# A two-block layer on one core: the first mixer reordered, its state-space chain ahead of the retention part

## The chip, the core and the metric

The kernel runs on one NeuronCore of a Trainium2 chip. A core has a matrix engine (TensorE, PE in the profile, with its weight loads as a row of their own, PEld), a vector engine (VectorE, DVE), an activation engine (ScalarE, ACT), a general engine (GpSimd, POOL) and a queue that issues DMAs (SyncE, SP). Each runs its own program in order, and they meet at semaphores. SBUF has 128 partitions and holds everything that is not in DRAM; products land in PSUM, eight banks of 128 x 512 float32. The metric is the time of one execution on the device in microseconds (us).

## The reference, cut to what matters

The whole is two transformer blocks over 1024 tokens of width 1024, in float32. Only the first block's mixer is touched in its order:

```python
h = x @ w_in                              # 1024 x 2048: u | q,k | v | gate, 512 columns each
# state-space part (s5): 32 groups of 16 channels, 64 complex states each
bu = einsum(u, b_bar);  states = scan(lam_bar, bu);  y = real(einsum(states, c)) + d * u
y = gelu(y);  y_s5 = rms_norm(y * sigmoid(y @ glu_w + glu_b))
# retention part: 4 heads, rotary q and k, a decayed state from chunk to chunk
y_ret = group_norm(intra + cross) * silu(gate)
mix = concat(y_s5, y_ret) @ w_out         # then layer norm, a conv-gated FFN, layer norm
```

After it come, unchanged, the first FFN and the second block (differential attention, two gated linear attentions, branch products, an FFN of 4096).

## The kernel before, in words

Every large product is done in three passes of reduced precision: an operand is cut into a high part (ACT, a copy to float32r) and a low part (POOL for weights, DVE for activations, a subtraction), and high x high, high x low and low x high are summed in PSUM. Weights come as 241 units of 128 x 1024 (512 KB) in the order of `weight_plan` (L52). A unit passes three places: SP loads it into a ring of NRAW = 3 raw slots (`load`, L2224), ACT cuts its high part (`act_cut`, L911, line L918) and POOL its low part (`pool_cut`, L2045, line L2050) into a ring of NSPL = 6 slots. Unit v may be cut when unit v - NSPL has been used up, and each program has its calls `act_cut(e, done)`, `pool_cut(e, done)` and `load(e, done)` at fixed places: they go up to unit done + NSPL (for `load` done + NSPL + NRAW).

A product is of one of two kinds. `pe_feature` (L371) turns one unit into 128 output features of all tokens: 48 matmuls of 128 x 512 into two banks. `pe_token_block` (L389) keeps four units at hand (two in the FFN's second half) and runs through the eight blocks of 128 tokens, 24 matmuls each; only in the last of the eight are its units given free. Banks are handed out round robin by `claim` (L353): whoever takes a bank waits until its last reader is done.

The first mixer runs in stages. `pe_in` (L419) makes u with four features and then three token blocks, qk, v and g (gate). DVE copies u out (L1388), and SP stores it to DRAM (`ubuf`). ACT copies qk and v out and applies silu to g, and all three stay in SBUF whole (QK, VV, GG, 16 KB of each partition each). Beside this DVE computes the state-space tables from L1393 on: exponentials and the angle arguments, on which ACT's two sines wait in order behind the eight copies of qk (L939, L940); powers PP, the input matrices BBR, and the rotation table ET.

Then comes `pe_retention` (L436) with `dve_retention` (L1466), a software pipeline of twelve steps: step n rotates q and k of chunk n on DVE (`keys`), turns them on PE (flip, L416), makes scores of chunk n - 1, outputs of chunk n - 2 (L460, L463) and the state's increment (L470); DVE masks (`masked`, L1502, L1507), updates the state (`state`, L1518), normalizes (`norm`, L1526 to L1540), and the result is turned (rt, L416) and cut into XH and XL (L1555).

After the last turn come `pe_s5` (L490), `dve_s5` (L1558), `act_s5` (L960), `pool_s5` (L2106) and `sp_s5` (L2256): DVE expands B by powers (M, BB, six operations of 128 x 2048), POOL does the same for C (C, CL, 24 operations of 128 x 576); PE turns B, injects u (L505), DVE rotates and scans (RTMP, WW) and rotates back (N, SS); PE makes the convolution kernel (L518), ACT copies it to KT, POOL adds d, SP spreads it into the Toeplitz tile T8 by eight DMAs (L2267); PE makes y with T8 and the states (`y8`, L530, L532), 24 matmuls in the program for each of four parts; ACT applies gelu, SP sends it through DRAM to turn its layout (`ybuf` L2271, YP L2274). Then the glu products (L367 with GH, GL), sums of squares (L554), the root and the scaling (L1626 to L1637). `pe_project_out` (L602) starts with the two weight units of the retention half (L618), so that the scaling of the state-space half runs beside it.

Of the kernel before, what the change touches and what calls it, by code (L numbers as in the profile page):

```python
# [7 lines left out]
F = mybir.dt.float32  # L8
# [8 lines left out]
NRAW = 3  # L17
NSPL = 6
KB = 1024
BASE = 1152 + 8 * KB  # L20
# [166 lines left out]
def build(nc, D, out):  # L187
    plan, order1, order2 = weight_plan()
    with ExitStack() as ctx:
# [3 lines left out]
        def sem(name):  # L193
# [14 lines left out]
        trig_arg, trig = sem("angles_reduced"), sem("sines_done")  # L208
        r_rot, r_qx, r_y, r_hi = (sem(n) for n in ("ret_rotated", "ret_query_scaled", "ret_normed", "ret_high_cut"))
        s_bk, s_cl, s_bb, s_et, s_t8z, s_kd, s_ss = (sem(n) for n in (  # L210
            "s5_b_kept", "s5_c_powers", "s5_b_powers", "s5_tables_read", "s5_toeplitz_zero", "s5_kernel_done", "s5_states"))
# [25 lines left out]
        WR = sb("WR", -8, [128, NRAW, 1024])  # L237
        WH = sb("WH", 4, [128, NSPL, 1024], R)
        WL = sb("WL", 28, [128, NSPL, 1024], R)
# [14 lines left out]
        U8 = sb("U8", 52, [128, 32, 128])  # L254
        QK = sb("QK", 148, [128, 8, 512])
        VV = sb("VV", 164, [128, 8, 512])
        GG = sb("GG", 180, [128, 8, 512])
        RT = sb("RT", 196, [128, R_N])
        GNG = sb("GNG", 202, [128, 512])
        TA = [sb(f"TA{j}", 84 + j, [128, 8, 32]) for j in range(4)]  # L260
        KQT = sb("KQT", 88, [128, 2, 4, 128])
        QX = sb("QX", 92, [128, 2, 2, 128])
        PT = sb("PT", 94, [128, 2, 4, 128])
        KZ = sb("KZ", 58, [128, 3, 256])
        SR = sb("SR", 52, [128, 2, 256])
        YR = sb("YR", 54, [128, 2, 512])

        ET = sb("ET", 116, [128, 16, 2, 128])
# [8 lines left out]
        CL = sb("CL", 148, [128, 16, 2, 144])  # L277
        BB = sb("BB", 166, [128, 16, 2, 128])
        SS = sb("SS", 84, [128, 16, 2, 128])
        BBT = sb("BBT", 182, [128, 16, 2, 128])  # L280
        KT = sb("KT", 84, [16, 32, 128])
        WW = sb("WW", 166, [128, 16, 2, 128])
        Y8 = sb("Y8", 116, [128, 32, 128])
        M1 = sb("M1", 84, [128, 16, 128])
        M2 = sb("M2", 92, [128, 16, 128])
        C1 = sb("C1", 142, [128, 4, 144])
        C2 = sb("C2", 144.5, [128, 4, 144])
        BK = sb("BK", 202, [128, 2, 16, 16])
        DM = sb("DM", 198, [16, 32])
        RTMP = sb("RTMP", 199, [128, 2, 2, 128])  # L290
        LAM = sb("LAM", 201.5, [128, 16])
        N1 = sb("N1", 182, [128, 16, 128])
        N2 = sb("N2", 190, [128, 16, 128])
        YP = sb("YP", 116, [128, 4, 1024])
        GH = sb("GH", 148, [128, 4, 1024], R)
        GL = sb("GL", 164, [128, 4, 1024], R)
        SG = sb("SG", 182, [128, 2, 1024])
        RS = sb("RS", 190, [128, 2, 1024])
# [90 lines left out]
        def pe_token_block(e, name, unit, col, row0, tiles, xh, xl, slots, after=None):  # L389
            vs = [wt.next(unit, row0 + 128 * k, 2, col, 512) for k in range(0, tiles, 2)]  # L390
            for i in range(8):
# [18 lines left out]
                u.units = wt.done  # L410
                if after:
                    after(i)

# [5 lines left out]
        def pe_in(e):  # L419
# [12 lines left out]
            pe_token_block(e, "qk", "w_in", 512, 0, 8, XH, XL, range(8))  # L432
            pe_token_block(e, "v", "w_in", 1024, 0, 8, XH, XL, range(8))
            pe_token_block(e, "g", "w_in", 1536, 0, 8, XH, XL, range(8))

        def pe_retention(e):  # L436
            def scores(i):
                d = i % 2
                f = lots["flip", i]
# [34 lines left out]
            for n in range(12):  # L474
# [4 lines left out]
                if n < 8:  # L479
                    u = claim(e, ("flip", n))  # L480
                    e.wait_ge(r_rot, n + 1)
                    if n == 0:
                        e.wait_ge(cst, 32)
# [6 lines left out]
        def pe_s5(e):  # L490
            for q in range(8):
                u = claim(e, ("bbt", q))
                if q == 0:
                    e.wait_ge(s_bb, 1)
# [2008 lines left out]
```

## Time and profile before

| | us |
|---|---|
| median of 3 runs | 3565.62 (3564.34 to 3565.73) |
| the profiled execution | 3569.1 |
| its span | 3567.2 |
| PE busy in the span | 3149.6 (88%) |
| PE on the chain that ended last | 80% |
| DVE on it | 9% |
| POOL busy | 996.8 (28%) |
| DVE busy | 1251.4 (35%) |

The profiled execution lies 3.5 us above the median. The profile's page cuts the span into 40 slices of 89.2 us. Its PE digits begin 8, 9, 5, 3, 5, 5, 8 and are 7 or more from there on, and the granted clock of TensorE falls to 5 tenths in the fifth and sixth of them. "Granted clock" is the share of full speed that the chip gave TensorE: 0.50 is 1.2 GHz, 1.00 is 2.4 GHz. Rows of the timeline begin with start and duration; what stands in brackets behind them is the idle time of the engine just before and what ended it. Where an operation's duration comes from a row with a count, it is the row's time by its count.

### The profile page before, as it was taken

To read this page: it belongs to the slowest core of one execution; us is meant where nothing else is said; L and a number is where in the kernel's file an instruction comes from. 1 tells how busy PE (TensorE), PEld (TensorE's weight loads), DVE (VectorE), ACT (ScalarE), POOL (GpSimd) and SP (SyncE) were. 2 spreads that over 40 slices of the span, in tenths; PEclk is the share of its full clock that TensorE was granted. 3 is DMA by queue.
4 is the path that set the end of the run, shared out by engine and by line. 5 is a ranking of instruction groups with operands and counts; after the bars stand their busy time and mean duration, and the time that the engine had idled before them with its cause. 6 is when DMAs were issued, how large, how long until landed. Compare 5 with 4: busy or idle time off the path is not lost.

```text
span 3567.2 us, 35327 instructions
## 1 busy us (share of the span) xinstructions
PE 3149.6 (88%) x14706; PEld 2578.5 (72%) x14706; DVE 1251.4 (35%) x2356; ACT 871.3 (24%) x1258; POOL 996.8 (28%) x446
## 2 busy tenths in 40 slices
PE   8953558999999998987899788799999999999995
PEld 7742346888888886665677677678887878888884
DVE  3567415321221225446345544511122511111115
ACT  2211012322112113333333444411112321111211
POOL 2214101543223234210133222212221453333332
PEclk9976569999999998998999999999999999999998
DMA  4102122111111111201111100022112111111101
GB/s 165 48 24 24 14 53 89 48 48 48 60 47 54 48 43 52 79 30 36 36 36 36 36 30 30 24 89 71 54 48 100 36 53 59 51 51 48 48 30 47
DMA packets 60351, 180.33 MB, mean 51 GB/s; under 512 B 9472, under 2 KB 18064, under 8 KB 60176
## 3 DMA queue, kind: packets, MB, share of 16 engines
q1 hardware_dynamic: 60192, 178.07, 16.2%
q8 instruction: 117, 1.92, 0.2%
q14 instruction: 42, 0.34, 0.0%
HBM read 157.99 MB, written 18.87 MB: 50 GB/s over the span
## 4 chain that ended last, share of the span: by engine, by line
PE 80%; DVE 9%; ACT 4%; issue 3%; POOL 3%; DMA 1%; SPq 1%; POOLq 0%; DVEq 0%; ACTq 0%
PE PS L367 44%; PE PS L400 7%; PE PS L402 7%; PE PS L401 7%; PE PS L578 3%; PE PS L818 2%; PE PS L416 1%; PE PS L707 1%; POOL WL L2050 1%; PE PS L532 1%; DVE s L1345 1%; PE PS L618 1%; POOL DD L2175 1%; PE PS L530 1%; PE PS L735 1%
## 5 line engine op out<-in xcount | busy, mean ns | idle before, releaser
L2050 POOL TENSOR_TENSOR WL<-WR,WH 128x1024 fp32r<-128x1024 f32 x241 | 579.1, 2410 | 2218.7 <-ACT WH L918 2218.4
L367 PE MATMUL PS<-XH,WH 128*128 128x512 f32 x2176 | 692.2, 400 | 15.0 <-DVE XL L1384 12.3
L367 PE MATMUL PS<-XL,WH 128*128 128x512 f32 x2176 | 679.0, 394 | 0.0
L367 PE MATMUL PS<-XH,WL 128*128 128x512 f32 x2176 | 674.9, 392 | 0.0
L367 PEld LDWEIGHTS PS<-XH,WH 128*128 128x128 f32 x2176 | 405.5, 191 | 103.9 <-issue 21.2
L367 PEld LDWEIGHTS PS<-XL,WH 128*128 128x128 f32 x2176 | 414.8, 191 | 88.5
L367 PEld LDWEIGHTS PS<-XH,WL 128*128 128x128 f32 x2176 | 412.4, 190 | 88.0
L918 ACT ACTIVATE WH<-WR 128x1024 fp32r<-128x1024 f32 x241 | 253.1, 1056 | 808.2 <-PE PS L402 475.0
L400 PE MATMUL PS<-WH,HH 128*128 128x512 f32 x864 | 339.5, 393 | 14.4 <-POOL HL L2082 14.4
L401 PE MATMUL PS<-WL,HH 128*128 128x512 f32 x864 | 338.7, 392 | 0.0
L402 PE MATMUL PS<-WH,HL 128*128 128x512 f32 x864 | 338.6, 392 | 0.0
L1723 DVE TENSOR_TENSOR XF<-XF,PS 128x512 f32<-128x512 f32 x192 | 132.0, 687 | 342.1 <-PE PS L402 342.1
L1707 DVE TENSOR_TENSOR CT<-CT,PS 128x1024 f32<-128x1024 f32 x54 | 66.0, 1221 | 459.1 <-ACT CT L1052 310.9
L400 PEld LDWEIGHTS PS<-WH,HH 128*128 128x128 f32 x864 | 164.1, 190 | 49.8 <-POOL HL L2082 15.7
L401 PEld LDWEIGHTS PS<-WL,HH 128*128 128x128 f32 x864 | 164.0, 190 | 34.2
L402 PEld LDWEIGHTS PS<-WH,HL 128*128 128x128 f32 x864 | 163.7, 189 | 34.3
L2082 POOL TENSOR_TENSOR HL<-CT,HH 128x1024 fp32r<-128x1024 f32 x54 | 129.4, 2396 | 16.1 <-ACT HH L1058 16.1
L400 PE MATMUL PS<-WH,XH 128*128 128x512 f32 x320 | 125.3, 392 | 4.9 <-POOL WL L2050 4.9
L402 PE MATMUL PS<-WH,XL 128*128 128x512 f32 x320 | 124.6, 389 | 0.0
L401 PE MATMUL PS<-WL,XH 128*128 128x512 f32 x320 | 124.5, 389 | 0.0
L818 PE MATMUL PS<-KQ 64*128 64x128 f32 (+1 forms) x896 | 89.4, 286 | 29.3 <-DVE KQ L1942 23.6
L818 PEld LDWEIGHTS PS<-KQ 64*128 64x128 f32 (+1 forms) x896 | 84.7, 198 | 38.8 <-issue 30.2
(317 smaller groups left out, 3819.0 us busy)
## 6 DMA issues: line engine op xcount, KB each, us to landing
WR<-in_weights SPq DMA_DIRECT2D x241, 512.0 KB, 3.6
BR<-brbuf SPq DMA_DIRECT2D x12, 512.0 KB, 4.7
RAWX<-in_xT SPq DMA_DIRECT2D x8, 512.0 KB, 9.3
RES<-in_x SPq DMA_DIRECT2D x8, 512.0 KB, 7.7
xbuf<-XF SPq DMA_DIRECT2D x8, 512.0 KB, 2.8
brbuf<-STG SPq DMA_DIRECT2D x8, 512.0 KB, 2.6
RES<-xbuf SPq DMA_DIRECT2D x8, 512.0 KB, 7.2
out<-XF SPq DMA_DIRECT2D x8, 512.0 KB, 2.6
```

The costliest lines, as they stand in the source:

```text
L367: last = e.matmul(PS[:, u.b + h, :], w, x[:, k, 512 * h:512 * h + 512], start=k == 0 and w is w1 and x is xh, stop=k == nk - 1 and w is w2)
L400: e.matmul(PS[:, u.b, :], a, wh[:, k, :], start=j == 0 and k == 0, stop=False)
L401: e.matmul(PS[:, u.b, :], a, wl[:, k, :], start=False, stop=False)
L402: last = e.matmul(PS[:, u.b, :], c, wh[:, k, :], start=False, stop=j == len(vs) - 1 and k == 1)
L416: last = e.transpose(PS[:, u.b, 128 * j:128 * j + 128], src(j), ident[:, :])
L578: last = e.matmul(PS[:, u.b + h, :], w[:, k, :], x[:, k, 512 * h:512 * h + 512], start=k == 0 and w is wh and x is XH, stop=k == 7 and w i ...
L818: last = e.matmul(PS[:, us[g][hh].b, 128 * (i % 4):128 * (i % 4) + 128], kl[rows[hh], c], kr[rows[hh], c], start=True, stop=True)
L918: e.activation(WH[:, v % NSPL, :], WR[:, v % NRAW, :], ACT.Copy).then_inc(w_hi, 1)
L1707: e.tensor_tensor(X, X, bank(u, 2), ALU.mult).then_inc(u.drained, 1)
L1723: e.tensor_tensor(x, x, bank(u), ALU.add).then_inc(u.drained, 1)
L2050: e.tensor_tensor(WL[:, v % NSPL, :], WR[:, v % NRAW, :], WH[:, v % NSPL, :].bitcast(F), ALU.subtract).then_inc(w_lo, 1)
L2082: e.tensor_tensor(HL[:, v % 5, :], CT[:, v % 2, :], HH[:, v % 5, :].bitcast(F), ALU.subtract).then_inc(f_lo, 1)
```

## The change

- The ring of cut weights has NSPL = 5 slots in place of 6, in the whole kernel. The 8 KB of each partition that come free hold two staging tiles (STQ), the retention tables and other small tiles.
- qk, v and g no longer stay in SBUF. ACT copies each block of 128 tokens into one of two slots of STQ, and SP stores it to DRAM (`spill`, 24 pieces of 256 KB). In the retention SP brings them back by chunks into QKC (2 slots), VVC (3) and GGC (2).
- In the start SP issues one weight unit ahead of x in place of three, and the state-space tables right behind x. ACT copies u out, and the sines follow the third part of u. DVE goes on from XL straight to the tables, BB (now in four groups of 128 x 512 operations) and ET; POOL expands C as soon as the powers are there (`pool_powers`).
- PE's program is one, `pe_mixer`: u, six token blocks of qk, four turns of B, a block, four turns, the last block; kernel and injection products with blocks of v between; the four y products with blocks of v between. B's turned form is written back over BB, and WW and SS use the same tile, so DVE works in place in groups; y is written over U8. The kernel goes to DRAM by quarters (`ktbuf`) and from there into T8.
- The retention pipeline runs last. In its steps lie the last two v blocks (step 0), the eight g blocks (steps 1 to 8), the glu products (steps 5, 6, 8, 9) and their squares (two steps later). DVE's order in a step is norm, keys, masked, the cut of rt, state. `norm` has 4 + 4 operations with the gain and the gate (tiles GNG and GGC) in place of 4 + 1, and the product of gate and gain over all eight blocks goes.
- `pe_token_block` is built on `pe_token_steps`, which yields after each token block; elsewhere it issues what it issued.

The core of the diff:

```diff
-NSPL = 6
+NSPL = 5
...
+            qk = pe_token_steps(e, "qk", "w_in", 512, 0, 8, XH, XL, range(8))
+            tick(qk, 6)
+            for q in range(4):
+                turn_b(q)
+            tick(qk, 1)
+            for q in range(4, 8):
+                turn_b(q)
+            finish(qk)
+            values = pe_token_steps(e, "v", "w_in", 1024, 0, 8, XH, XL, range(8))
+            kernel_of(0)
+            inject(0)
+            inject(1)
+            kernel_of(1)
+            tick(values, 1)
+            kernel_of(2)
+            kernel_of(3)
+            for q in range(2, 8, 2):
+                inject(q)
+                inject(q + 1)
+                if q < 6:
+                    tick(values, 1)
+            for q in range(4):
+                outputs(q)
+                if q < 3:
+                    tick(values, 1)
...
+                if n == 0:
+                    finish(values)
+                else:
+                    tick(gates, 1)
+                if n in glu_at:
+                    p = glu_at[n]
+                    if p % 2 == 0:
+                        glu_units.append(wt.next("s5_glu_w", 0, 4, 128 * p, 256))
+                    glu(p)
+                if n - 2 in glu_at:
+                    squares(glu_at[n - 2])
+        glu_at = {5: 0, 6: 1, 8: 2, 9: 3}
...
+        def act_spill(e, name, i, func=ACT.Copy):
+            s = 8 * ("qk", "v", "g").index(name) + i
+            if s >= 2:
+                e.wait_ge(spilled[s % 2], 16 * (s // 2))
+            act_evac(e, lots[name, i], STQ[:, s % 2, :], func=func)
...
+            def kernel_of(p):
+                u = lots["kt", p]
+                k = KTS[p % 2]
+                if p >= 2:
+                    e.wait_ge(kt_out[p % 2], 16)
+                elif p:
+                    e.wait_ge(s_et, 1)
...
+            s = lots["y8", 3]
+            e.wait_ge(s.full, s.nfull)
+            qk(0)
+            qk(1)
+            e.wait_ge(s.drained, s.ndrained)
...
         def vector_program(e):
             dve_in(e)
+            dve_s5(e)
             dve_retention(e)
-            dve_s5(e)
```

The first `kernel_of` is PE's, the second ACT's: ACT's copy of the second quarter waits for `s_et`, the end of ET on DVE, since its tile lies over ET's scratch.

## Rows read from the trace of the kernel before

**Rows 1.** Windows: bounds, length, busy us (count) of PE, PEld, DVE, ACT, POOL; granted clock.

```profile
196.00:317.00 121.00, 52.75 (x252) 42.35 (x252) 94.45 (x317) 13.30 (x20) 10.38 (x5) 0.69 0.06 18
317.00:336.00 19.00, 0.10 (x1) 0.14 (x2) 18.76 (x8) 0.63 (x1) 18.54 (x6) 0.50 1.16 97
...
414.00:474.00 60.00, 59.66 (x192) 45.55 (x192) 0.08 (x1) 3.26 (x6) 0.00 (x0) 0.50 0.00 1
```

**Rows 2.** Waits of PE, 196 to 600 us: sum, times, longest.

```profile
PE PS L530 <- DVE SS L1613: 33.9, 1, 33.9
PE PS L367 <- DVE GL L1616: 27.5, 1, 27.5
```

**Rows 3.** Timeline of DVE, from the third part of u to the first rotation.

```profile
47.69 2.03 DVE L1388 COPY UP<-PS 128x1024 f32<-128x1024 f32 x1 [8.84 <-PE PS L367]
...
112.47 0.07 DVE L1410 MEMSET PP<- 128x16 f32 x1 [40.64 <-ACT LL L940]
...
123.76 0.29 DVE L1345 COPY BBR<-E 128x256 f32<-128x256 f32 x1
...
127.35 0.23 DVE L1345 MEMSET ET<- 128x16 f32 x2 [0.16 <-DVE LL L1345]
...
150.44 2.74 DVE L1345 TENSOR_TENSOR ET<-ET,E 128x512 f32<-128x512 f32 x1
...
158.42 2.88 DVE L1372 TENSOR_TENSOR E<-ET,LL 128x512 f32<-128x512 f32 x1
...
164.24 0.43 DVE L1345 COPY ET<-E 128x512 f32<-128x512 f32 x1
...
196.68 0.42 DVE L1345 TENSOR_TENSOR TA<-QK,RT 128x256 f32<-128x256 f32 x1
```

**Rows 4.** Timeline of ACT, a cut of x, a block of qk, the table load before the sines.

```profile
11.11 1.06 ACT L932 ACTIVATE XH<-RAWX 128x1024 fp32r<-128x1024 f32 x1 [0.21 <-DMA RAWX<-in_xT]
...
69.45 0.60 ACT L922 ACTIVATE QK<-PS 128x512 f32<-128x512 f32 x1 [4.84 <-PE PS L402]
...
110.79 1.28 ACT L939 ACT_TABLE_LOAD   x1
```

**Rows 5.** Timeline of POOL, four weight cuts, then the expansion of C.

```profile
149.87 10.89 POOL L2050 TENSOR_TENSOR WL<-WR,WH 128x1024 fp32r<-128x1024 f32 x4 [36.62 <-ACT WH L918]
...
317.23 3.32 POOL L2115 TENSOR_TENSOR C<-BCT,PP 128x576 f32<-128x576 f32 x1 [110.00 <-DVE XL L1555]
...
337.09 1.22 POOL L2115 TENSOR_TENSOR C<-BCT,PP 128x576 f32<-128x576 f32 x1
```

**Rows 6.** Timeline of DVE, the expansion of B, one group of scans, the rotation back.

```profile
322.73 3.18 DVE L1345 TENSOR_TENSOR BB<-M,M 128x2048 f32<-128x2048 f32 x1
...
343.57 0.42 DVE L1345 TENSOR_TENSOR RTMP<-PS,ET 128x256 f32<-128x256 f32 x1 [6.53 <-PE PS L505]
...
363.01 1.80 DVE L1345 TENSOR_TENSOR_SCAN WW<-LAM,WW 128x128 f32<-128x128 f32 x4
...
400.14 0.09 DVE L1345 MEMSET SS<- 128x32 f32 x1 [12.92 <-DMA T<-KT]
400.26 4.58 DVE L1345 TENSOR_TENSOR N<-WW,ET 128x2032 f32<-128x2032 f32 x2
```

**Rows 7.** Timeline of SP, the eight DMAs that fill T8 (issue).

```profile
384.79 8.95 SPq L2267 DMA_DIRECT2D T<-KT  x8
```

**Rows 8.** Timeline of DVE, two steps of the retention.

```profile
262.63 0.69 DVE L1555 TENSOR_TENSOR XL<-PS,XH 128x512 fp32r<-128x512 f32 x1 [1.97 <-ACT XH L958]
...
268.41 0.89 DVE L1526 BATCH_NORM_STATS2 s<-PS 128x6 f32<-128x128 f32 x4
```

**Rows 9.** Timeline of PE, a sum of squares, the projection's first product.

```profile
514.35 3.78 PE L554 MATMUL PS<-SG,ones 128*128 128x512 f32 x4 [5.06 <-DVE SG L1622]
...
560.40 1.42 PE L618 MATMUL PS<-WH,XH 128*128 128x512 f32 x1
```

**Rows 10.** Waits of PE from 100 to 200 us.

```profile
PE PS L400 <- POOL WL L2050: 4.9, 4, 1.8
```

More of the change, by code:

```diff
@@ L410, in pe_token_block @@
                 u.units = wt.done
+                yield
+        def pe_token_block(e, name, unit, col, row0, tiles, xh, xl, slots, after=None):
+            steps = pe_token_steps(e, name, unit, col, row0, tiles, xh, xl, slots)
+            for i in range(8):
+                next(steps)
                 if after:
                     after(i)
+            next(steps, None)
         def pe_turn_four(e, u, src):
@@ new lines, in inject @@
+            def inject(q):
+                t = lots["bbt", q]
+                e.wait_ge(t.drained, t.ndrained)
+                if q == 0:
+                    e.wait_ge(u8_in, 128)
+                u = claim(e, ("inj", q))
+                for j in range(4):
+                    gp, ri = 2 * q + j // 2, j % 2
+                    for g2 in range(2):
+                        last = e.matmul(PS[64 * g2:64 * g2 + 64, u.b, 128 * j:128 * j + 128],
+                                        BB[:, gp, ri, 64 * g2:64 * g2 + 64], U8[:, 2 * gp + g2, :], start=True, stop=True)
+                last.then_inc(u.full, 1)
@@ new lines, in kernel_of @@
+            def kernel_of(p):
+                u = claim(e, ("kt", p), 2)
+                e.wait_ge(s_cl, p + 1)
+                for gp in range(4 * p, 4 * p + 4):
+                    for g2 in range(2):
+                        rr, c0 = slice(64 * g2, 64 * g2 + 64), 128 * (gp % 4)
+                        for ri in range(2):
+                            last = e.matmul(PS[0:16, u.b + g2, c0:c0 + 128], BBR[rr, ri, gp, :], CL[rr, gp, ri, 0:128],
+                                            start=ri == 0, stop=ri == 1)
+                last.then_inc(u.full, 1)
@@ L934, in act_in @@
             for p in range(4):
[L935 to L944 removed]
+                u = lots["u", p]
@@ L1624, in dve_s5 @@
+                if 2 <= n < 9:
+                    state(n - 2)
+                if n == 4:
+                    for p in range(4):
+                        e.wait_ge(g_hi, p + 1)
+                        e.tensor_tensor(GL[:, p, :], YP[:, p, :], GH[:, p, :].bitcast(F), ALU.subtract).then_inc(g_lo, 1)
+                if n - 1 in glu_at:
+                    glu(glu_at[n - 1])
+            r0, r1, r2 = (RS[:, k, :] for k in range(3))
             u = lots["ss"]
@@ L2278, in sp_s5 @@
+            load(e, lots["g", 7].units)
+            load(e, lots["glu", 3].units)
+            e.wait_ge(g_sum, 4)
+            e.wait_ge(lots["ro", 7].full, lots["ro", 7].nfull)
             for i in range(8):
```

630 lines of the change are left out of this document (329 added, 301 removed).

## The prediction

> **What bounds the kernel now.** I read the profile's page first: PE is busy 88% of the span and carries 80% of the chain that ended last, so the kernel as a whole is bound by matmuls that the change doesn't touch. The exception is the first mixer: the page's digits for PE sink to 3 to 5 there and the granted clock with them. Then I read the windows by stage [rows 1]: in the 121 us of the retention PE works 52.8 us, in the 19 us in which DVE and POOL expand B and C it works 0.1, and in the 60 us of the y products it works all the time, but at a granted clock of 0.50. The waits of PE name the two longest idle stretches [rows 2]: 33.9 us for DVE's rotation and the Toeplitz tile, 27.5 us for y on its way through DRAM. The projection starts at 560.4 [rows 9]. Its own tail (root and scaling beside the two retention units) is the same before and after, so what the change is worth is how much earlier the projection's first product comes, less what the ring of five costs behind it.
>
> What could stand in that time: the 24 token blocks of qk, v and g take 5.44 us each (0.60 busy and 4.84 idle of ACT's copy [rows 4]), 131 us, and in the kernel before nothing but DVE's tables runs beside them. The retention and the state-space part are independent of each other. So the gain has a source: in one, DVE's chain of the state-space part moves beside qk and v; in the other, g, glu and the squares move into the retention, whose steps leave PE half idle.
>
> **Start.** x arrives in pieces 1.27 us apart (1.06 busy and 0.21 idle for one cut of x [rows 4]), each the size of a weight unit. Two weight units move behind x: everything starts 2 x 1.27 = 2.5 us earlier. The third part of u is complete at 47.7 before [rows 3], so at 45.2; ACT's strided copy is put at DVE's 2.0 us for it [rows 3], a weight cut at 1.1, the table load at 1.3 [rows 4], two sines at 0.4: DVE has the sines at about 50 in place of 112.5. It waited 40.6 us for them before [rows 3], because they stood behind the copies of qk on ACT; its argument work of some 11 us ends by 35 and is hidden.
>
> **Tables, B and C.** From the sines to BBR DVE takes 112.5 to 124.05 [rows 3], 11.6 us: done at 61.6. POOL first cuts unit 8 (which waits for the last part of u) and begins C at about 62. Then DVE's 24 operations of 128 x 512 and POOL's 24 of 128 x 576 run at once, and both read two operands from SBUF. The rows show what that costs: DVE's BB takes 3.18 us beside POOL and 2.29 alone for nearly the same size (4.58 for two [rows 6]), and POOL's C takes 3.32 beside DVE and 1.22 alone [rows 5]. They take turns: a pair takes about 3.2, 0.3 less than the sum of both alone. For a pair here I take 0.7 + 1.3 - 0.25 = 1.75 us, 42 us for all 24, with ends of 17 (DVE undisturbed, 24 x 0.72) and 47 (24 x 1.95, the full sum). BB is ready at 103.5. PE has done six blocks of qk by 89 and waits for the third and fourth group of B, up to about 8 us, which is hidden as long as DVE is the later one.
>
> The Trainium skill says the same more strictly, in SBUF — State Buffer, section "SBUF: two separate sides": a DVE operation with two SBUF inputs and a GpSimd operation exclude each other for their whole length. By it the pair is the full sum, 47 us in place of 42, 5 us more in the result. It speaks against putting DVE's and POOL's expansions side by side with ET behind them.
>
> The end of ET: squarings 3.3 us (124.05 to 127.35) and ET from 127.35 to 164.67 [rows 3], 37.3 us, of which four weight cuts of POOL took some 8.4 us (four operations from 150.44 to 158.42 took 2.5 to 2.9 us where the same forms take 0.4 to 0.7 [rows 3, 5]). The cuts of v's units, behind the last block of qk, fall into ET again, so I keep 37.3. **ET ends at E = 103.5 + 3.3 + 37.3 = 144.**
>
> **From E to y.** A group of the scans costs DVE 4.4 us (six operations at 0.42 and scans 1.80 [rows 6]), the rotation back of two groups six operations at 0.7: 8 x 4.4 + 4 x 4.4 = 53 us, the last at E + 53. The Toeplitz tile is later at first: ACT's second kernel copy waits for E and stands ahead of v's first copy; PE's fourth kernel quarter takes the banks of the first two injections (E + 5.5 to E + 9 at half clock); copy, d, store to DRAM (about 2 us each) end at E + 14; POOL clears T8 (3.5 us), SP stands behind the store of v's second block (E + 21), and from the first of the eight issues to landing it took 400.1 - 384.8 = 15.4 us [rows 6, 7]: T8 is there at E + 37. Then four y products with three v blocks between. Before they take 15 us each, at a clock of 0.50 throughout [rows 1]. The v blocks raise the clock (token blocks run at 5.44 us, full clock). I take 15 for the first, 11 for the others, between 7.5 and 15, and 6.5 for a v block: 15 + 33 + 19.5 = 67.5. **y is complete at E + 105 = 249**; the first chunk is fetched only then (its tile lies over C), 3 us: the retention starts at 252 in place of 196.7.
>
> The Trainium skill, TensorE: Matmul & The Clock Gate, the section on the HAM clock gate, says that activity releases the throttle. By it a stretch as busy as y's would run at the full clock, 30 us for the four and not 48, 18 us less in the result. The trace disagrees: 59.66 of 60 us busy at 0.50 [rows 1]. A v block between them is new, so that price is open on both sides.
>
> **The retention.** Before it takes 196.7 to 317.2 [rows 3, 5], 121 us, a step 13.6 us (249.07 to 262.63 [rows 8]), bound by DVE, with 2 us of idle for the turned result. Added: (1) the last two v blocks ahead of the first scores (10.9) and the first g block, which waits for units cut only after them, while SP, in `load`, waits for the same cuts and holds back the third chunk of qk (4), less 4 that hides: 11. (2) `norm` has three more operations on 128 x 128, +0.9 us per step for eight steps, mostly given back by the new order, which leaves no idle for the turned result: 5. (3) GL, four operations of 1.24: 5. (4) glu gates and squares on DVE, 8 of 1.24: 10. (5) PE's steps with g (5.4), glu (5.4) and squares (3.8 [rows 9]) pass DVE's 14 us in five steps, by some 2 to 4: 12. (6) six more weight cuts beside DVE, 2 us each: 9. Sum 52: **172 us, the projection at 252 + 172 = 424** in place of 560.4, 136 us earlier. Spills add 24 stores and 24 loads of 256 KB to SP; each wait there (a store behind ACT's copy, a chunk behind `state` or `norm`) is a step ahead of its use, so I cost them at nothing beyond (1); without that cover each chunk costs about 3 us, 24 us in eight steps.
>
> **The ring of five.** It counts in the whole kernel. At the starts of v and g PE waited 4.9 us in all for low cuts [rows 10], since a block gives its four units free only at its end. One slot less brings that to about 2.5 us where there was just enough: the second half of the first projection, one feature of the last FFN's start. Elsewhere, holding each cut's end against the unit's first use, the cut after it would still be in time by over 2 us. I take 5 us, between 0 and 15.
>
> **Sum.** 3569.1 - 136 + 5 = 3438 for an execution like the profiled one. That lies 3.5 us above the median, which I keep as the difference: **3435 us.**
>
> **The rivals.**
> (a) The gain is larger: DVE is less disturbed by POOL (up to 25), T8 isn't last, y runs at full clock (18), the retention costs 25 less since PE's extra work hides. Half of that: 3435 - 50 = 3385. For it speaks that PE is half idle in the retention; against it that pairs take turns in every row.
> (b) The retention becomes bound by PE at half clock or by SP's chunks: eight g steps at 20 us for 14, 48 us, and y at 15 throughout (12): 3495. For it speaks the clock of 0.69 in the retention [rows 1]; against it that g blocks keep PE dense.
> (c) Slower than before: the ring of five. If each change between token blocks behind the mixer (28 in the two FFNs, 4 in the projections) waited for a cut as v and g do, at 2.5 us, that would be 80 us; the sign turns where each costs 131 / 32 = 4.1 us or more, at 6 us 3620. Against it: an FFN block has two units, and three slots stay ahead.
> (d) The change doesn't do what it says: DVE runs in order, and the retention can't begin before the scans end. If the state-space chain took as long as before from the start of B (317 to 474, 157 us, from 62), y would be complete at 219 and not later: so order alone can't undo it. Its price is inside (b).
>
> **How the numbers follow.** Forecast 0.60, (a) 0.17, (b) 0.19, (c) 0.03, no change that can be told 0.01. About 0.2% is what a measurement of this kernel can tell from none. The forecast's own bounds: B and C -25/+5, y -18/+12, retention -25/+30, ring -5/+10, added as independent: -40/+35. The range goes on to (a) and halfway to (b): 3385 to 3485. Faster 0.96, same 0.01, slower 0.03.
>
> **What would show it.** Right: the first projection product at 415 to 435; the sines at 50; the last ET copy at about 144; BB operations at 0.7 busy but 1.7 apart; PE idle from about 120 to 145 and again before y; T8 landed near 180; y complete near 250; steps of 14 to 16 us. Wrong: y products at 7.5 us (a); steps of 20 us or DVE waiting for chunks (b); PE waiting on WL in the FFNs (c). If PE's waits behind the projection grew by over 15 us, or the projection began beyond 460, the sum is wrong.

## The result, and the profile after

| | before | after |
|---|---|---|
| median | 3565.51 us (3564.34 to 3565.73) | 3409.55 us (3408.32 to 3412.85) |
| the profiled execution | 3569.1 | 3408.3 |
| its span | 3567.2 | 3406.2 |
| mean granted clock of the profiled execution | 0.935 | 0.958 |

The changed kernel takes 0.9565 of the time of the one before (95% interval 0.9548 to 0.9581), 156 us less. The forecast was 3435 us with a range of 3385 to 3485: the time lies in it, 25 us below the forecast.

The page of after; its slices are 85.2 us long, the first five of them hold the mixer:

```profile
PE 3110.5 (91%) x14706; PEld 2549.1 (75%) x14706; DVE 1263.8 (37%) x2407; ACT 880.2 (26%) x1265; POOL 990.4 (29%) x450
...
PE   8688899999999979878997887899999999999995
...
PEclk9789999999999989988999999899999999999998
```

The 3, 5, 5 of PE and the 6, 5, 6 of its clock are gone. (On the page of before only the fifth slice stands at 5 tenths of the clock, the sixth at 6, and PE's last digit is a 5.) PE runs the same 14706 matmuls, and its busy time fell by 39 us, of 161 in the span, at a granted clock that rose from 0.935 to 0.958: the other 122 us are idle time that is no longer there.

DVE's chain in after. Rows begin with start and duration; this view is the timeline, as in [rows 3, 6]:

```profile
48.69 0.07 DVE L1483 MEMSET PP<- 128x16 f32 x1 [9.03 <-ACT LL L983]
...
63.84 1.40 DVE L1423 COPY BBR<-E 128x256 f32<-128x256 f32 x1
65.28 3.30 DVE L1423 TENSOR_TENSOR M<-BBR,PP 128x512 f32<-128x512 f32 x2
68.61 1.81 DVE L1423 TENSOR_TENSOR BB<-M,M 128x512 f32<-128x512 f32 x1
...
101.01 1.42 DVE L1423 TENSOR_TENSOR M<-BBR,PP 128x512 f32<-128x512 f32 x2
102.47 0.69 DVE L1529 TENSOR_TENSOR BB<-M,M 128x512 f32<-128x512 f32 x1
```

Then, from the same view of the later stretch, the rotation's end and the first two rotations of the retention:

```profile
195.64 0.69 DVE L1594 TENSOR_TENSOR BB<-M,M 128x508 f32<-128x508 f32 x1
...
237.93 0.42 DVE L1423 TENSOR_TENSOR TA<-QKC,RT 128x256 f32<-128x256 f32 x1 [41.60 <-DMA QKC<-spill]
...
271.29 0.42 DVE L1423 TENSOR_TENSOR TA<-QKC,RT 128x256 f32<-128x256 f32 x1 [15.13 <-DMA QKC<-spill]
```

The wait for the sines, 40.6 us in [rows 3], is 9.0. B takes 65.3 to 103.2, and its last three operations, when POOL's C has ended (100.4), show the operation undisturbed: 0.69 to 0.71 us in place of 1.6 to 1.8. The rotation back ends at 196.3, 52 us behind the end of ET (the forecast had 53). The first rotation stands at 237.9, after the wait for y that lets the first chunk be fetched.

The waits of PE from 100 to 420 us (sum, times, longest), to be held against [rows 2, 10]:

```profile
PE PS L466 <- issue: 25.0, 1, 25.0
PE PS L421 <- DVE KZ L1623: 12.6, 3, 5.8
PE PS L533 <- DVE YR L1668: 8.1, 2, 6.4
...
PE PS L479 <- DMA T<-ktbuf: 6.0, 1, 6.0
```

The 25.0 us "issue" is the fourth kernel quarter (line 466), which stands for the banks of the first two injections; DVE empties them only behind ET, the second by 150.8. The 33.9 us before y of [rows 2] are 6.0.

The windows of the y products of after, with the columns of [rows 1]; the first, a v block, then product, block, product, block, product, and the retention:

```profile
177.00:192.00 15.00, 14.86 (x48) 11.40 (x48) 14.03 (x32) 0.00 (x0) 0.00 (x0) 0.50 0.00 1
192.00:199.00 7.00, 7.00 (x27) 5.66 (x26) 4.12 (x8) 1.09 (x2) 0.00 (x0) 0.82 0.00 0
199.00:207.00 8.00, 8.00 (x48) 6.19 (x46) 0.00 (x0) 0.60 (x1) 0.00 (x0) 1.00 0.10 35
207.00:213.00 6.00, 6.00 (x29) 4.84 (x27) 0.00 (x0) 1.10 (x3) 0.00 (x0) 1.00 0.00 0
213.00:221.00 8.00, 8.00 (x47) 6.22 (x46) 0.00 (x0) 0.58 (x1) 0.00 (x0) 1.00 0.09 33
...
238.00:398.00 160.00, 128.81 (x603) 101.42 (x604) 111.60 (x352) 41.78 (x51) 23.61 (x10) 0.91 0.37 112
```

The first product takes 15 us at 0.50 as in [rows 1], the others 8.4 at 1.00. y is complete at 235.1. The end of the mixer on PE, where 398.41 answers to 560.40 in [rows 9]:

```profile
395.62 3.78 PE L567 MATMUL PS<-SG,ones 128*128 128x512 f32 x4 [1.81 <-DVE SG L1683]
398.41 1.27 PE L662 MATMUL PS<-WH,XH 128*128 128x512 f32 x1
```

The projection starts 162.0 us earlier. From there to the end of the span the kernel before needed 3567.2 - 560.4 = 3006.8 us and this one 3406.2 - 398.4 = 3007.8.

### The profile page after: what moved, and what is told of

Same layout as the page of the kernel before. It is cut to its first block, busy times and chain, and to the rows that moved or that the text cites. A ratio compares the mean times of both kernels' runs of the same rounds, so it can differ in the third digit from the quotient of the medians.

```text
span 3406.2 us, 35503 instructions
## 1 busy us (share of the span) xinstructions
PE 3110.5 (91%) x14706; PEld 2549.1 (75%) x14706; DVE 1263.8 (37%) x2407; ACT 880.2 (26%) x1265; POOL 990.4 (29%) x450
## 4 chain that ended last, share of the span: by engine, by line
PE 79%; DVE 10%; ACT 4%; issue 3%; POOL 3%; DMA 1%; SPq 0%; POOLq 0%; DVEq 0%; ACTq 0%
PE PS L365 45%; PE PS L398 7%; PE PS L399 7%; PE PS L400 7%; PE PS L622 3%; PE PS L862 2%; PE PS L751 1%; POOL WL L2134 1%; DVE s L1423 1%; DVE M L1423 1%; PE PS L481 1%; PE PS L421 1%; POOL DD L2260 1%; PE PS L662 1%; PE PS L779 1%
## 5 line engine op out<-in xcount | busy, mean ns | idle before, releaser
L365 PE MATMUL PS<-XH,WH 128*128 128x512 f32 x2176 | 692.2, 400 | 11.7 <-DVE XL L1462 9.0
L365 PEld LDWEIGHTS PS<-XH,WH 128*128 128x128 f32 x2176 | 405.5, 191 | 100.5 <-issue 17.8
L1785 DVE SCALAR_TENSOR_TENSOR CT<-PS,cols,CT 128x1023 f32<-128x1023 f32 x22 | 28.2, 1283 | 238.3 <-ACT CT L1123 238.3
```

The source lines that it names most:

```text
L365: last = e.matmul(PS[:, u.b + h, :], w, x[:, k, 512 * h:512 * h + 512], start=k == 0 and w is w1 and x is xh, stop=k == nk - 1 and w is w2)
```

## The experiments

Each is given with its time, and, from its profiled execution, the start of the projection (398.4 in after) and what else its verdict rests on. "Less" and "slower" compare medians; "after" is the changed kernel. The interval of a ratio is some 10 us wide, and for the edits worth under 7 us (sines_early, chunk2_early, glu_small) it overlaps that of after: their verdicts rest on the rows of one trace each.

### The ring of five, alone and with a second dose

In the kernel before (ring5; ring4 has 4 in the same place):

```diff
-NSPL = 6
+NSPL = 5
```

> The kernel before, with a ring of five cut weights and nothing else changed. Theory: only the places where there was just enough wait more (v, g, the second half of the first projection), 2.5 us each: +2 to +7 us on 3565.5, since behind the first projection's start the changed kernel needed 3007.8 us where the one before needed 3006.8. Rival (c) of the prediction: each change between token blocks waits 2.5 us or more, +80 us and up. If it comes out below +1 us, the term of 5 us in the sum was a loss that isn't there.

> The kernel before with a ring of four, a second dose. A token block of a projection holds four units to its end, so with four slots no unit of the next one can be cut ahead: load is done, but ACT's cut (1.06 us) and POOL's (2.4 us) of the first unit stand open, 3.5 us and more at each such block, and more where an FFN's feature and block meet. Theory (five is just above the point where it begins to cost): some tens of us, 30 to 120, against +2 to +7 for five. Rival (slots don't matter at all, units are cut late for other reasons): under 10 us.

Measured: ring5 3575.46 us, ratio 1.0027 (1.0017 to 1.0038), so +6 to +14 us; ring4 3598.48, ratio 1.0095 (1.0081 to 1.0109), +29 to +39. The waits of PE behind POOL's low cuts over the whole span, first of ring5, then of ring4:

```profile
PE PS L400 <- POOL WL L2050: 10.7, 8, 2.7
```

```profile
PE PS L400 <- POOL WL L2050: 13.4, 7, 4.4
PE PS L578 <- POOL WL L2050: 13.0, 2, 6.5
```

In the kernel before they are 4.9 over the whole span, those of [rows 10]. In ring5 the projection starts at 564.3, 3.9 later than before, and 3.6 us are added behind it; in ring4 8.1 and 21.2. So the slot isn't free. Its price by the medians is 10, above the 2 to 7 expected and above the 5 in the sum (7.5 in these two executions), half of it lies ahead of the projection, and the second slot less costs two to three times as much (23 by the medians). Rival (c), 80 us and more, falls. None of these waits of ring5 is longer than 2.7 us.

### v's blocks ahead of y

```diff
-            for q in range(4):
-                outputs(q)
-                if q < 3:
-                    tick(values, 1)
+            tick(values, 3)
+            for q in range(4):
+                outputs(q)
```

ACT's copies stand in the same order.

> The changed kernel with v's blocks 3 to 5 ahead of the first y product in place of between the four. Theory A (what TensorE did right before decides the clock: a y product that follows a token block keeps 1.00, one that follows an idle gap stays at 0.50 to its end): PE fills the 6.0 us wait for the Toeplitz tile, y runs 4 x 8.3 us right behind at 1.00 and is complete near 224.5 in place of 235.1: 3399 us, 10.6 less than 3409.6. Theory B (dense y products by themselves let the clock fall, and it was the blocks between them that brought it back): the second to fourth take 15 us, y complete near 244, +9 us: 3418. Theory C (the retention doesn't wait for y): no change.

Measured: 3396.02 us, ratio 0.9529 (0.9516 to 0.9542), 13.5 less than after; y complete at 221.8, the projection at 385.5. Windows over the four products, back to back (all have 1.00):

```profile
187.00:196.00 9.00, 9.00 (x52) 6.99 (x51) 8.41 (x19) 1.88 (x2) 0.00 (x0) 1.00 0.08 31
196.00:205.00 9.00, 9.00 (x53) 6.94 (x52) 0.70 (x2) 1.19 (x3) 0.00 (x0) 1.00 0.00 0
...
213.00:221.80 8.80, 8.77 (x51) 6.64 (x50) 0.00 (x0) 1.08 (x2) 0.00 (x0) 1.00 0.01 2
```

34 us of the same matmuls that ran 60 us at 0.50 in [rows 1] keep 1.00 here. Theory A holds (it had 3399), B falls, and C too: 13.3 us of y are 13.0 at the projection. What was gained is the 6.0 us wait for the Toeplitz tile and the slow first product.

### The kernel quarters early

```diff
-        KTS = [sb("KTS0", 198, ...), sb("KTS1", 142, [16, 8, 128])]
+        KTS = [sb("KTS0", 198, ...), sb("KTS1", 208, [16, 8, 128])]
...
-                elif p:
-                    e.wait_ge(s_et, 1)
+                elif p:
+                    e.wait_ge(s_cl, 4)
```

and PE, ACT and SP take the four quarters ahead of the injections, of v's first copy and of its first store; RT and GNG are loaded behind T8.

> The changed kernel with all four kernel quarters ahead of the injections on PE, the second staging tile of the quarters off the place of E1 (so that ACT doesn't wait for the end of ET), and the retention's tables loaded behind the Toeplitz tile. Theory: the tile is then cleared right behind ET (144.2 + 3.5), its eight loads land 14.4 us after that, at 162 in place of 177.1 (E + 18 for E + 33), PE's idle stretch of 25 us is filled from both ends, the first y product still follows a gap (15 us at 0.50), y is complete 15 us earlier, near 220, total 3395. Rival: y is paced by DVE's scans (the four groups end at 157, 170, 183, 196), then the last y product starts at 196 or later and the gain is the same, but with v's blocks between not full. Other rival: the loads of T8 meet the spills and take longer; gain under 8 us.

Measured: 3397.63 us, ratio 0.9533 (0.9519 to 0.9548), 11.9 less than after. The first y product starts at 163.9 in place of 177.1, behind an idle time of 7.0 us, and runs at 0.50; y is complete at 222.5, the projection at 387.0. T8 is cleared right behind ET (144.5 to 148.0) and its loads are issued from 148.0, in place of 162.8. In after T8 was the later of the two things that y needs, as the prediction had it: DVE's first rotation back is done at 157.4, and PE's wait is for T8. In kernel_early the first product is let go by a third thing, the bank of an injection that DVE empties at 163.8, so more than 13 us could not come of this edit.

Three things tied T8 to a late time in after: ACT's second copy waited for the end of ET (144.2) because of its staging tile, PE's fourth quarter waited until 150.8 for the banks of the injections, and SP stood behind the store of v's second block until 162.7. The edit takes away all three at once; what the tile alone is worth was not tried, and with the tile alone the fourth quarter would still have waited for the banks.

### DVE's chain, from its two ends

```diff
-                if p == 2:
+                if p == 1:
                     e.wait_ge(trig_arg, 1)
```

> The changed kernel with ACT's two sines behind the second part of u in place of the third. Their argument is ready at 39.7, ACT waits for it and has copied the second part by then, so the sines come at 41.3 in place of 48.6, 7.3 us earlier. Theory (DVE's one chain of tables, BBR, B, ET, scans sets the end of the mixer): E falls from 144.2 by 7.3 to 11 (the expansion of BBR then no longer meets POOL's C, which starts at 60.8 for another reason), y complete 227 in place of 235, total 3399 to 3402. Rival (the end of B is set by POOL's C at 100.4, since both take turns on SBUF): B ends at the same 103, no gain, 3409.

Measured: 3402.78 us, ratio 0.9547 (0.9531 to 0.9563), 6.8 less than after; ET ends at 137.9 (144.2 in after), the projection starts at 392.5. Of E's 6.3 us 5.9 arrive: the chain is on the path, and E gained a little less than the 7.3 to 11 expected. But on the way more was won and lost again. The sines come 8.3 us earlier, BBR and B's first six operations are done before C begins (61.3, set by a weight cut), and B ends at 88.6 in place of 103.2, 14.6 us earlier. DVE's timeline behind B in this kernel:

```profile
91.24 2.70 DVE L1423 TENSOR_TENSOR LL<-LL 128x16 f32<-128x16 f32 x4
...
98.03 1.30 DVE L1423 SCALAR_TENSOR_TENSOR LL<-LL 128x16 f32<-128x16 f32 x1
99.36 0.38 DVE L1423 TENSOR_TENSOR LL<-LL 128x16 f32<-128x16 f32 x2
```

The squarings, operations of 16 columns and 0.17 to 0.19 us, take up to 1.3 us each until C ends at 99.3: they last 11.2 us in place of 3.1. So 8.1 of the 14.6 us are given back. The end of POOL's C is a second bound, as the rival had it, only not a hard one.

Then POOL's C, cut to its first group (y leaves out the others' terms):

```diff
+                if g:
+                    e.memset(CL[:, gg, :, :], 0.0).then_inc(s_cl, 1)
+                    continue
                 e.tensor_tensor(c1, cw(2), cp(PP[:, 0, :, :]), ALU.mult).then_inc(pool, cg.up())
```

> The changed kernel without POOL's C powers for three of the four groups of channels: CL of these is cleared to zero, so y leaves out their kernel and state terms (the work of every other engine is the same). It prices what POOL's C costs DVE's chain. Theory (their operations take turns on SBUF, as the pairs of 1.70 us show, where B's operation takes 0.71 alone): B's 24 operations take 17 to 22 us in place of 38, BBR's last four operations 1.8 in place of 6; E falls from 144.2 to about 122, y complete 20 us earlier, total 3388 to 3392. Rival A (B is paced by its own waits between dependent operations, POOL is innocent): B stays at 38 us, E and the total the same within 3 us. Rival B (B gets faster, but PE's qk blocks and T8 are the next bound): E falls by 20, y by less than 8.

Measured: 3392.57 us, ratio 0.9518 (0.9504 to 0.9532), 17.0 less; ET ends at 126.8, the projection starts at 382.1. DVE's timeline in this kernel, B's first group, in the middle of which (at about 71) POOL's C ends:

```profile
65.71 3.30 DVE L1423 TENSOR_TENSOR M<-BBR,PP 128x512 f32<-128x512 f32 x2
69.04 1.81 DVE L1423 TENSOR_TENSOR BB<-M,M 128x512 f32<-128x512 f32 x1
70.89 1.42 DVE L1423 TENSOR_TENSOR M<-BBR,PP 128x512 f32<-128x512 f32 x2
72.34 0.69 DVE L1529 TENSOR_TENSOR BB<-M,M 128x512 f32<-128x512 f32 x1
```

B takes 20.4 us in place of 37.9. B's operations that meet POOL's take 0.9 to 1.1 us more; both rivals fall, since 17.4 us of E give 17.0 in the time. The expected 22 was too much because C's first group stayed, and with it BBR's slow end.

### The third chunk of qk

```diff
-                if 1 <= n < 7:
+                if 2 <= n < 7:
                     qk(n + 1)
...
                 if n == 0:
+                    qk(2)
                     sp_spill(e, "v", 6)
```

> The changed kernel with SP's fetch of qk's third chunk ahead of the stores of v's last two blocks and ahead of the weight loads behind them, in place of behind them. In the changed kernel DVE waits 15.1 us for this chunk near 269. Theory (the wait is on the retention's path, as the prediction has it with 4 us for it): the projection starts 4 to 11 us earlier, total 3399 to 3406. Rival (PE is late there too: it turns the chunk's forerunner and runs v's last blocks and g's first one in order, so a fetch that is in time only moves the wait to PE): under 2 us.

Measured: 3405.70 us, ratio 0.9553 (0.9539 to 0.9567), 3.8 less; the projection starts at 396.2, 2.2 earlier. DVE's wait falls from 15.1 to 5.6, PE's wait for KZ by 4.1, and the rest comes back in other places (DVE's waits for ACT's XH grow by 2.4). That is at the foot of the theory's range, between it and the rival. Of 9.5 us less waiting on DVE some 2 to 4 were on the path, in line with the prediction's 4; the kernel's own runs spread by 3 to 5 us, so the size isn't known better.

### What bounds the retention

Two doses on the added glu. On DVE (the gates and squares of most columns are left out):

```diff
-                e.tensor_tensor(YP[:, p, :], YP[:, p, :], SG[:, a, :], ...)
+                e.tensor_tensor(YP[:, p, 0:64], YP[:, p, 0:64], SG[:, a, 0:64], ...)
...
-                e.tensor_tensor(SG[:, a, :], YP[:, p, :], YP[:, p, :], ...)
+                e.tensor_tensor(SG[:, a, 0:64], YP[:, p, 0:64], YP[:, p, 0:64], ...)
```

> The changed kernel, with DVE's eight gating and squaring operations of the glu (128 x 1024, 1.24 us each by the kernel before) cut to 64 columns; most of y is then not gated. It prices term (4) of the prediction's sum for the retention, 10 us. Theory (the retention is bound by DVE, each operation added to DVE lengthens it): the projection starts 8 to 9 us earlier, total near 3401. Rival (in the steps with glu, n from 5 to 9, PE's turn, scores, glu and gate block are the longer part and DVE waits for them anyway): under 3 us.

On PE (three quarters of the glu's contraction are left out):

```diff
-                for k in range(4):
-                    last = pe_slice(e, u, wh, wl, GH, GL, k, 4, 128 * (p % 2))
+                last = pe_slice(e, u, wh, wl, GH, GL, 0, 1, 128 * (p % 2))
```

> The changed kernel, with the four glu products of PE contracted over one slice of the four (6 matmuls of 24 each), so the gates are not those of the reference; DVE's and ACT's work is unchanged. It takes 3 x 1.36 us off each of four steps of PE, 16 us at full clock. It prices term (5) of the prediction's sum for the retention, 12 us (PE's step passes DVE's in five steps). If PE bounds these steps to the full: 16 us less, total 3394. By the prediction's sum, an overhang of 2 to 4 us a step: 8 to 12 us less, 3398 to 3401. If DVE bounds them: under 3 us.

Measured: glu_small 3402.61 us, ratio 0.9550 (0.9536 to 0.9564), 6.9 less than after, and the retention (first rotation to projection) 152.8 us in place of 160.5. glu_short 3408.87 us, ratio 0.9566 (0.9550 to 0.9582), the same as after, and the retention 160.4. The waits of PE in the retention of glu_short:

```profile
PE PS L421 <- DVE KZ L1622: 13.1, 4, 5.7
PE PS L533 <- DVE YR L1667: 12.0, 2, 6.3
PE PS L517 <- issue: 7.8, 3, 3.6
```

In after the three are 12.6, 8.1 and 3.2. PE's busy time fell by 10.6 us, not 16, as its granted clock in the stretch was 0.85 in place of 0.91; 9.0 of them are back as longer waits in these three rows. The retention is DVE's: 8 operations less are worth 7.6 us of their 9.3 (15/16 of 8 x 1.24), the PE work taken out is worth nothing.

### Versions put together

> The changed kernel with four edits at once: sines behind u's second part, the kernel quarters ahead of the injections with their second tile off E1's place, v's blocks 0 to 5 all ahead of the first y product (two between each pair of injections), chunk 2 of qk fetched earlier. Theory: E at 135, T8 landed at 153, PE dense through v to about 164, four y products at 1.00 (8.6 us each, 34 us), the last not before DVE's scans end (E + 52 = 187): y complete near 200 in place of 235.1, total 3409.6 - 35 - (0 to 6) = 3368 to 3375. Rival (gains overlap: both single edits took the same idle stretch of PE, 13 us each): y complete near 215, total 3388 to 3392.

The edits are those above, with PE in the order: four kernel quarters, two injections, v 0 and 1, two injections, v 2 and 3, four injections, v 4 and 5, four y products.

Measured: ratio 0.9472 (0.9450 to 0.9494), a median of 3376.75 us between runs of 3369.8 and 3370.1 and others of 3383.4 and 3384.9. The profiled execution is one of the latter: ET ends at 139.4, y starts at 167.8 and is complete at 213.5, the projection at 371.4. Windows over its y products:

```profile
176.00:184.60 8.60, 8.60 (x51) 6.56 (x49) 7.98 (x20) 1.08 (x2) 0.00 (x0) 1.00 0.00 0
186.00:187.00 1.00, 1.00 (x7) 0.82 (x6) 0.93 (x3) 0.00 (x0) 0.00 (x0) 0.79 0.00 0
187.00:188.00 1.00, 1.00 (x5) 0.78 (x4) 0.96 (x3) 0.00 (x0) 0.00 (x0) 0.50 0.00 0
```

Ahead of the third product PE was idle for 0.34 us (until 185.03; it stands at the claim of a bank, which an injection held), and from 187 the clock is 0.50 to the end of y: 13.8 and 14.7 us for two products that take 8.4 at 1.00. That is 11.7 us. The faster runs have a mean clock of 0.964 in place of 0.959, a difference of about the size that 28.5 us at half the clock make in the whole; that they kept the clock is likely and not shown, as there is no trace of them. Against after the gain is 33 us by the median, 25 and 40 by its two kinds of runs, where the theory had 35 to 41 and the four single gains sum to 36: in the faster runs the edits add up, in the slower ones some 12 us are missing, and the trace has them in the clock.

> As the combined kernel, but in another order on PE: three injections, v's blocks 0 to 4, five injections, v 5, y 0, y 1, v 6, y 2, v 7, y 3, so that all eight v blocks lie ahead of the retention, and two of them between y products that in the combined kernel ran dense and fell to 0.50 in the profiled run. Theory: E near 139, PE is no longer blocked by banks before E, y 0 starts near 158 to 160, all y products at 1.00 (8.4 us), y complete near 203 (213.5 in the profiled combined run, whose last two products took 14 us each), the retention's start is free of v 6 and v 7 (10.9 us of PE), the projection starts near 353 in place of 371.4: 3360 to 3368, and its runs lie within 4 us of each other, where those of the combined kernel split at 3370 and 3384. Rival A (the clock falls in dense y whatever stands between): y complete 213, spread as before, 3372 or more. Rival B (the retention is bound by DVE from its first step, v 6 and v 7 were free in it): the projection starts at 358 or later, 3368 to 3372.

Measured: 3372.05 us, ratio 0.9461 (0.9447 to 0.9475), runs from 3370.4 to 3372.4. It is the fastest of all kernels run, 37.5 us less than after, and yet above the 3360 to 3368 of its theory. All four y products run at 1.00, none behind a gap, and the runs lie within 2 us of each other: rival A falls. But y starts at 164.2 (PE had waited 7.5 us for a bank) and is complete at 208.9, and the first rotation stands at 218.0, 9.1 us behind that (2.8 in after). The timeline of SP (issues) in this kernel shows why:

```profile
150.22 51.50 SPq L2343 DMA_DIRECT2D spill<-STQ  x6
204.78 7.58 SPq L2311 DMA_DIRECT2D WR<-in_weights  x4
212.47 1.12 SPq L2370 DMA_DIRECT2D QKC<-spill  x2
213.65 11.80 SPq L2385 DMA_DIRECT2D ybuf<-U  x8
```

SP stood in the weight loads behind v's last block, which wait for POOL's cuts, while the chunks waited: 3.6 us, and the first chunk then took 5.5 us from its issue to the rotation in place of 2.8, with those loads in flight. The retention takes 144.0 us in place of 160.5. In the profiled execution of combined, with the third chunk earlier but v 6 and v 7 still in the first step, it took 154.8; so of the 16.5 some 11 are the two blocks and some 6 the chunk (roughly, since combined also entered the retention at the lower clock). Rival B's reason, that the two blocks were free there, falls, though its numbers (the projection at 358 or later, 3368 to 3372) came out: the projection starts at 362.0, by the late start of y and of the first chunk.

> As v_inside, with three faults of its trace mended. (1) SP stood in the weight loads behind v 7 from 204.8 to 212.5, waiting for POOL's cuts, so the first chunk of qk was asked for 3.6 us after y; the loads now stand behind the first chunks, and ACT cuts the fifth unit only behind y's copies. (2) PE waited 7.5 us for the bank of the third injection: now two injections stand before v's blocks 0 to 5 and six behind, v 6 ahead of y 0, v 7 between y 1 and y 2. (3) The third chunk of qk goes between the eight stores of y (11.8 us of SP), the first chunk of v ahead of them; in v_inside DVE waited 6.5 us for it. Theory: y 0 starts near 160, no product at 0.50, y complete near 200 in place of 208.9, the first rotation at 203 in place of 218.0, the projection starts near 345 to 348 in place of 362.0, total 3356 to 3360 in place of 3372. Rival (y 3 waits for DVE's last scans at 190.8, the clock falls in that gap): y complete 206, total 3364. Other rival (DVE's pace in the retention takes back what the third chunk gave): 3362.

Measured: 3376.96 us, ratio 0.9472 (0.9459 to 0.9485), 4.9 us slower than v_inside and 17 to 21 above its theory; the projection starts at 367.3. The three faults are gone and three others have come. Windows over the first product and the start of the second:

```profile
162.00:170.90 8.90, 8.90 (x51) 6.78 (x49) 8.31 (x20) 1.88 (x2) 0.00 (x0) 1.00 0.08 29
172.20:174.00 1.80, 1.80 (x10) 1.43 (x10) 1.66 (x5) 0.00 (x0) 0.00 (x0) 0.88 0.01 5
174.00:176.00 2.00, 2.00 (x8) 1.55 (x8) 1.97 (x4) 0.00 (x0) 0.00 (x0) 0.50 0.00 0
```

With two injections ahead and six behind, the second product's banks are those of injections that DVE empties only at 172; the gap of 1.27 us is followed by the fall to 0.50, which lasts to the product's end, and the v block behind it brings the clock back (8.4 us for the last two). y is complete at 210.6. The retention starts earlier, at 213.3, but takes 154.0 us in place of 144.0: ACT's fifth weight cut, now in front of its first turned copy, waits until 220.9 for a load (PE then waits 5.2 us for that copy), and PE waits 2.8 us for a chunk of v and DVE 6.1 us for one of g.

## Why the prediction was right, step by step

Right in what it rests on: the token blocks fill with DVE's chain, and PE's idle time at the y chain and behind it goes. The profiled execution was predicted at 3438 and took 3408.3; the difference of 30 us is 26 at the start of the projection (424 against 398.4) and 4 behind it. By the median it is 25, since the forecast took the profiled execution to lie 3.5 us above the median as before, and it lay 1.2 below. The two larger misses, y and the retention, lie on the same side.

- **Start, tables, B and ET.** Sines at 48.6 (forecast 50), BBR at 65.2 (61.6), B 37.9 us (42), ET's end at 144.2 (144). The last is exact by luck, since errors cancel: the row for BBR was taken without POOL beside it, and from the sines to BBR it took 16.6 us, not 11.6, beside a weight cut and POOL's C, against sines 1.4 us earlier; a pair took 1.58 us on the mean, not 1.75 (1.70 in the middle groups, and the last three operations ran alone). That POOL's C and DVE's B slow each other is shown: no_c_powers takes 17.5 us off B. The full sum of 0.71 and 1.22 per pair, which the Trainium skill's rule gives (SBUF — State Buffer, "SBUF: two separate sides"), would be 1.93; the middle groups show 1.70, 0.23 less, so they don't keep each other out for their whole recorded length, and the measurement decides.
- **T8.** Landed at 177.1 (forecast 181), last of the two, as said; kernel_early, which has it earlier by three changes at once, shows that its lateness cost at least 12 us.
- **y, 14 us too late in the forecast.** The sum had 15 + 3 x 11 + 3 x 6.5 from 181. Measured: 15, 3 x 8.4, and three blocks in 17.8. The term that was mis-sized is the choice of 11 between 7.5 and 15: a product behind a token block ran at the full clock for its whole length and took 8.4, near the low end (halving 15 gave 7.5, which no product reached). 8 of the 14 us are this, 4 are T8's earlier landing, 2 the blocks. The rows of before had token blocks at full clock and y at half, each by itself, and nothing of one behind the other. The Trainium skill's rule (TensorE: Matmul & The Clock Gate, the HAM clock gate), by which activity releases the throttle, gave 18 us less. For the first product it failed again (14.86 of 15 us busy at 0.50); the other three ran at the full clock, as by the rule (8.4 us), but behind token blocks. In v_first all four did.
- **The retention, 12 us too long in the forecast** (172 against 160.5). The term that failed is (5), 12 us for PE's steps being longer than DVE's: glu_short takes 4 us off PE in each of four of these steps and nothing changes, so there PE's steps don't pass DVE's. (4) was 10, glu_small gives 7.6 for all but a sixteenth of it. (1) was 11, and v_inside, without v 6 and v 7 and with an earlier third chunk, takes 16.5 off: too small by up to 5, and what was too small is the chunk (some 2 to 6, where the sum lets its 4 hide), not the two blocks (some 11, in the sum 10.9). (2), (3) and (6) together would then be about 15 in place of 19; they weren't taken apart, and two of them don't follow from their own words: six cuts of 2 us are 12 and stand as 9, and of 0.9 x 8 = 7 us "mostly given back" 5 are charged. The granted clock of 0.91 in the retention refutes rival (b), which needed half.
- **The stores and loads of the chunks**, costed at nothing. ACT's waits from 50 to 110 us in after show a long one:

```profile
ACT STQ L965 <- DMA spill<-STQ: 24.2, 2, 22.8
```

SP stands in the loads of U8 until 75.4, the first blocks of qk wait to be stored behind them, and so ACT has no free slot for the third block until 89.3; PE, with eight banks ahead of it, lost 0.56 us by that. So it was the banks that hid this wait. The cover that the prediction names, a step between each transfer and its use, held in the retention of after but for the third chunk, which the sum has in (1). v_inside2 shows how thin it is at the retention's start: there one weight load that came late made PE wait 5.2 us for ACT's first copy.
- **The ring.** 5 in the sum; 7.5 in ring5's execution against that of before, 6 to 14 by the ratio, and of this the four ahead of the projection are in the mixer's times above. Behind it, 1.0 in after, where ring5 has 3.6; why these differ is open.
- **Rivals.** (a) came true in two of its parts, y at full clock for three products and PE's extra work hidden, and not in DVE being less disturbed; by size the result lies midway between forecast and (a). Its size was loosely set: the parts with a price sum to 68 (25, 18 and 25), half of which is 34 and not 50, and T8's part has none. (b), (c) and (d) fell.

## What to carry to other kernels

A chain of one engine that runs beside another's dense work is priced by three things that its own duration doesn't show: what stands ahead of its first operand in the other queues (two sines behind one copy less: 6 us), what another engine does on SBUF beside it (17 us for POOL's C), and which tiles, banks and queues tie it to its neighbours (12 us for a staging tile, an order of banks and a place in SP's queue). In an order with banks handed out in turn, a bank held by a slow reader stops everything behind it (25.0 us of PE in after), and each move shifts who meets it: v_inside2 mended three waits and met three others. Before adding up engine times for an interleaved loop, give each engine its own sum and take only what is added to the longest: 16 us of PE's work were worth nothing here, 9.3 us off DVE 7.6.

## What the runs showed of the hardware

TensorE's granted clock doesn't follow from its busy share. The same y products, with PE busy all the time, run at 0.50 (60 us in [rows 1], 15 us in after behind 6.0 us of idle, the same in kernel_early behind 7.0) and at 1.00 (34 us in v_first, behind token blocks). Where they ran at 1.00 and PE stood still for a moment, the clock fell: 0.34 us of idle in combined and 1.27 us in v_inside2 were each followed within 2.0 us by 0.50, which then lasted until a token block came; in v_first and v_inside no gap stood between products and the clock never fell. This is two cases against two, and whether the gap is the cause wasn't tried by itself; the two faster runs of combined suggest that it isn't certain to happen. A gap alone is not enough: in the profiled execution of combined PE stands still for 1.52 and 0.67 us between the matmuls (128 x 512) of g's first block, and the clock stays at 1.00:

```profile
232.00:240.00 8.00, 5.81 (x31) 4.00 (x30) 1.07 (x3) 3.44 (x4) 5.03 (x3) 1.00 0.95 349
```

A y product at 0.50 costs 5.4 to 6.6 us more than one at 1.00.
